# Four edits to a two-layer transformer kernel: a moved Silu, a projection that waits tile by tile, dots ahead of expert turns, and squares added in pairs

## The chip, the core and the metric

The kernel runs on one core of one Trainium2 chip. The metric is the device time of one execution in microseconds (us); lower is better. Everything is one launch, in fp32, with all inputs in HBM.

## The reference, cut

Two different transformer layers run one after the other on 256 tokens of width 1024. Each is modulated by a vector c: `silu(c) @ w_ada` gives shifts, scales and gates.

```python
# layer 1
sh1, sc1, gt1, sh2, sc2, gt2 = split(silu(c) @ w_ada + b_ada, 6)
proj = (rms_norm(h, norm1_g) * (1 + sc1) + sh1) @ w_in
...                                        # an attention (o_moba) and a recurrence (o_rwkv)
g_moba, g_rwkv = split(sigmoid(gate_logits), 2)
mixed = g_moba * (o_moba @ w_proj_moba) + g_rwkv * (o_rwkv @ w_proj_rwkv)
h = h + gt1 * (mixed @ w_out)
xn2 = rms_norm(h, norm2_g) * (1 + sc2) + sh2
h = h + gt2 * peer_ffn(xn2, ...)           # 8 heads choose 16 of 16384 experts per token:
                                           # gelu(x . u_e) * gate, times v_e, summed
# layer 2
shift_a, scale_a, gate_a, shift_f, scale_f, gate_f = split(silu(c_2) @ w_ada_2 + b_ada_2, 6)
h2 = rms_norm_2(x, attn_norm) * (1 + scale_a) + shift_a
...                                        # h2 @ w_in_2, two attentions, w_o, a convolved ffn
```

## The kernel before, in words

Five engines run queues that are written out by hand, in order: TensorE (`pe_...` functions), the Vector engine (`dve_...`), ScalarE (`act_...`), GpSimd (`pool_...`) and SP, which issues nearly all loads (`sp_...`). They meet in semaphores; `wait_ge` blocks the queue of its engine and `then_inc` raises a semaphore when the instruction is done. [...]

Weights come as tiles of 128 x 1024 in a ring of six slots (`wring`). Most products are made in three matmuls: ScalarE casts the upper half of a weight tile (L491, `whi`), the Vector engine or GpSimd subtracts it to get the lower half (L496, `wlo`), and TensorE multiplies upper by upper, upper by lower and lower by upper (L502 to L504). `tile_done` counts tiles that TensorE has finished, in one order for the whole program; `ring_free` counts PSUM banks (three in a ring) that have been read.

The places that the change touches, in the order of time:

- **Gates.** TensorE makes 16 gate tiles, the last of them beside the end of the recurrence. For each, ScalarE takes a sigmoid of the bank (L1340) and then casts the weight tile three further on. `act_rwkv_out` (L1719) does the last five; ahead of them it takes a square root (L1722) and the Silu of `crow` (L1726), the broadcast of c. Sqrt, Silu and Sigmoid each need a table load when they change. GpSimd subtracts for gate tiles 14 and 15.
- **Projections and output projection.** `pe_proj` makes eight tiles (L1742), `dve_proj` multiplies them with the gates and adds the two halves into `mix1` (L1762, L1764), and beside that takes dots of rows of `w_ada` with `crow` (L1781). `pe_w_out` waits until all eight tiles of `mix1` are there and then makes eight tiles (L477).
- **Experts.** All 16384 experts are computed densely, as 128 pairs of tiles: an up tile (L515 and L523, 16 + 8 matmuls) gives hidden values, and a down tile (L2106 to L2110, 12 matmuls) uses them. Up tiles 0 to 39 were made early. From j = 40 on a turn j is, on TensorE, up(j) and then down(j-1). On the Vector engine it is `turn(j)`: subtract the next up tile's lower half (L496), add the two parts of the hidden values (L2233), wait for ScalarE's Gelu, multiply by the gates (L2238), subtract the lower half of down tile j (L496), and subtract the lower part of W (L2226), which down(j) waits for. Turns 40 to 126 are two hardware loops of three turns each round; turn 127 stands alone.
- **Dots of layer 2's modulation.** Its 96 half rows (128 x 512, 256 KB) are loaded one by one into one buffer (`rG["half"]`, in `xn`), and the Vector engine takes a dot of each with crow2 (L2246, then a copy, L2249). `half(u)` waits for the landing of half u and gives the buffer free (`half_free`). Nine of them lie in the early down turns, the others one in each turn of the loops, u = 9 with j = 40 and so on. SP's queue in the loop (`sp_peer`) is, per turn, two weight tiles and one half:

```python
for u in range(SLOTS):
    tile(first + SLOTS + u, i)               # waits until the tile six back is done
    if u % 2:
        half(lone + u // 2 + 1, i)           # waits for half_free of the dot before
```

  Half 9 stands ahead of the loop, behind the weight tile that waits for down(38); half 10 behind the one that waits for down(39), and so on.
- **First norm of layer 2.** After the last down tile the residual is added in eight steps; for each, ScalarE writes the upper raw tile (L661) and a square (L547), the Vector engine the lower raw tile (L671), and TensorE takes six raw matmuls (two weight tiles of `w_in2`) and one norm matmul that sums the square over partitions into bank 4 (L576). Its result goes through a square root on ScalarE (L592) into all that follows. At the second norm of each layer GpSimd already adds squares (`pool_squares`, L567).

## Time and profile before

| | us |
|---|---|
| median of 3 runs | 1642.43 |
| lowest and highest run | 1640.56, 1642.7 |
| the profiled execution | 1641.95 |
| its span, first to last instruction | 1640.2 |
| TensorE busy in the span | 1599.8 (98%) |
| Vector engine busy | 1263.5 (77%) |
| ScalarE busy | 869.3 (53%) |
| GpSimd busy | 194.8 (12%) |

The expert loop, from 673 to 1156 us, is the longest stretch with one pattern. The gates end near 261 us, the two projections near 318, and the first norm of layer 2 lies from 1165 to 1176. In the views a row of the timeline is one group of equal instructions: start, duration, engine, line and operation; in brackets stands how long the engine was idle before it and what ended that.

### The profile page before, as it was taken

Reading aid. Unit: us, or ns where it says so; the run is one execution under the profiler, and the core shown is the slowest. Engines: PE = TensorE matmul, PEld = TensorE weight load, DVE = VectorE, ACT = ScalarE, POOL = GpSimd, SP = SyncE. Lnnn points to the kernel's source line nnn. Section 1 sums busy time; section 2 is a strip of 40 time slices with the busy share of each in tenths; the row PEclk is TensorE's granted clock in tenths of the full one; section 3 lists DMA queues with packets and bytes.
Section 4 is the critical chain, followed back from the end, with each engine's and each line's share of the span. In section 5 each row is a group of like instructions: output and inputs, shape, how many; then the busy total and the mean of one; then the engine's idle time right before and its main releaser. Section 6 shows DMA issues by size and latency. Waiting matters only on the chain.

```text
span 1640.2 us, 32822 instructions
## 1 busy us (share of the span) xinstructions
PE 1599.8 (98%) x11530; PEld 1421.0 (87%) x11530; DVE 1263.5 (77%) x2680; ACT 869.3 (53%) x1599; POOL 194.8 (12%) x153
## 2 busy tenths in 40 slices
PE   6999999999999999999999999999999999999998
PEld 4887988899988878888888888888899877999998
DVE  6885547859989978787888888888778465688887
ACT  3444221365469944555555555555654245566665
POOL 0020211017700000000000000000048004300000
PEclk9999999999999999999999999999999999999999
DMA  9842136855742288777767777777545561255553
GB/s 357 292 140 87 40 118 220 333 192 172 229 131 65 89 261 266 231 236 238 238 233 242 234 240 236 238 239 241 187 156 169 200 215 40 77 170 185 184 180 129
DMA packets 102625, 316.92 MB, mean 193 GB/s; under 512 B 11392, under 2 KB 21376, under 8 KB 102144
## 3 DMA queue, kind: packets, MB, share of 16 engines
q1 hardware_dynamic: 101664, 311.27, 57.2%
q10 hardware_dynamic: 864, 4.32, 0.7%
q8 instruction: 65, 1.06, 0.3%
q14 instruction: 32, 0.26, 0.0%
HBM read 309.65 MB, written 5.90 MB: 192 GB/s over the span
## 4 chain that ended last, share of the span: by engine, by line
PE 80%; ACT 7%; DVE 6%; POOL 2%; issue 2%; DMA 2%; SPq 0%; DVEq 0%; POOLq 0%; ACTq 0%
PE bank L515 10%; PE bank L502 9%; PE bank L503 8%; PE bank L504 8%; PE bank L2106 7%; PE bank L2108 7%; PE bank L2110 7%; PE bank L523 5%; POOL wlo L496 2%; ACT arena L2069 2%; PE bank L763 2%; PE bank L1624 2%; PE bank L1742 2%; ACT arena L2060 2%; PE bank L1325 1%
## 5 line engine op out<-in xcount | busy, mean ns | idle before, releaser
L491 ACT CAST whi<-wring 128x1024 fp32r<-128x1024 f32 x395 | 412.7, 1046 | 177.0 <-PE bank L504 109.6
L496 DVE TENSOR_TENSOR wlo<-wring,whi 128x1024 fp32r<-128x1024 f32 x341 | 416.9, 1223 | 63.8 <-ACT whi L491 55.0
L496 POOL TENSOR_TENSOR wlo<-wring,whi 128x1024 fp32r<-128x1024 f32 x54 | 138.1, 2564 | 910.3 <-ACT whi L491 910.3
L502 PE MATMUL bank<-xboth,whi 128*128 128x256 f32 x752 | 219.3, 292 | 6.8 <-POOL wlo L496 2.6
L503 PE MATMUL bank<-xboth,whi 128*128 128x256 f32 x752 | 212.6, 283 | 0.0
L504 PE MATMUL bank<-xboth,wlo 128*128 128x256 f32 x752 | 212.6, 283 | 0.0
L515 PE MATMUL bank<-xboth,whi 128*128 128x512 f32 x704 | 188.7, 390 | 0.0
L2106 PE MATMUL bank<-whi,Whi 128*128 128x512 f32 x512 | 159.7, 393 | 3.2 <-DVE Wlo L2226 3.2
L2108 PE MATMUL bank<-wlo,Whi 128*128 128x512 f32 x512 | 158.6, 391 | 0.0
L2110 PE MATMUL bank<-whi,Wlo 128*128 128x512 f32 x512 | 157.7, 389 | 0.0
L502 PEld LDWEIGHTS bank<-xboth,whi 128*128 128x128 f32 x752 | 143.9, 191 | 13.7 <-issue 6.4
L515 PEld LDWEIGHTS bank<-xboth,whi 128*128 128x128 f32 x704 | 132.5, 188 | 24.0
L502 PE MATMUL bank<-raw,whi 128*128 128x258 f32 x504 | 144.7, 287 | 2.9 <-DVE raw L671 1.4
L503 PEld LDWEIGHTS bank<-xboth,whi 128*128 128x128 f32 x752 | 144.1, 192 | 0.8 <-issue 0.7
L504 PEld LDWEIGHTS bank<-xboth,wlo 128*128 128x128 f32 x752 | 144.0, 191 | 0.0
L503 PE MATMUL bank<-raw,whi 128*128 128x258 f32 x504 | 142.8, 283 | 0.0
L504 PE MATMUL bank<-raw,wlo 128*128 128x258 f32 x504 | 141.5, 281 | 0.0
L2106 PEld LDWEIGHTS bank<-whi,Whi 128*128 128x128 f32 x512 | 95.2, 188 | 22.1 <-issue 2.9
L2110 PEld LDWEIGHTS bank<-whi,Wlo 128*128 128x128 f32 x512 | 96.1, 188 | 21.0
L2108 PEld LDWEIGHTS bank<-wlo,Whi 128*128 128x128 f32 x512 | 96.1, 188 | 21.0
L2179 ACT ACTIVATE arena<-arena 128x256 f32<-128x256 f32 x88 | 36.8, 418 | 128.1 <-DVE arena L2233 128.1
L523 PEld LDWEIGHTS bank<-xboth,wlo 128*128 128x128 f32 x704 | 96.0, 190 | 6.9
(397 smaller groups left out, 3111.7 us busy)
## 6 DMA issues: line engine op xcount, KB each, us to landing
wring<-in_w SPq DMA_DIRECT2D x463, 512.0 KB, 4.1
arena<-in_ada SPq DMA_DIRECT2D x48, 512.0 KB, 7.4
xn<-in_ada SPq DMA_DIRECT2D x96, 256.0 KB, 2.8
h_spill<-arena SPq DMA_DIRECT2D x37, 128.0 KB, 2.0
arena<-h_spill SPq DMA_DIRECT2D x37, 128.0 KB, 3.8
wring<-in_w SPq DMA_DIRECT2D x6, 384.0 KB, 6.0
wring<-in_w SPq DMA_DIRECT2D x8, 256.0 KB, 3.2
arena<-in_const ACTq DMA_DIRECT2D x1, 1151.0 KB, 5.3
```

The source lines that it names most:

```text
L491: act.copy(whi[:, n % HSLOTS, :], wring[:, n % SLOTS, :]).then_inc(hi_ready, 1)
L496: eng.tensor_tensor(wlo[:, n % SLOTS, :], wring[:, n % SLOTS, :], whi[:, n % HSLOTS, :].bitcast(F32), ALU.subtract).then_inc(lo_ready, 1)
L502: pe.matmul(out, h, xh, start=start, stop=False, **kw)
L503: pe.matmul(out, h, xl, start=False, stop=False, **kw)
L504: return pe.matmul(out, l, xh, start=False, stop=stop, **kw)
L515: return pe.matmul(out, whi[:, n % HSLOTS, k * 128:k * 128 + 128], xboth[:, k, :, :], start=(k == 0), stop=(k == KT - 1))
L523: pe.matmul(out[:, 0:S], wlo[:, n % SLOTS, k * 128:k * 128 + 128], xhi[:, k, :], start=False, stop=False)
L763: mm = pe.matmul(bk[:, at:at + w], q[:, b * 128:(b + 1) * 128], k[:, 0:w], start=(i == 0), stop=(i == len(j["q"]) - 1))
L2106: pe.matmul(tok_accs[b][f][:, :], Wh, h[:, f * 512:(f + 1) * 512], start=first, stop=False)
L2108: pe.matmul(tok_accs[b][f][:, :], Wh, l[:, f * 512:(f + 1) * 512], start=False, stop=False)
L2110: mm = pe.matmul(tok_accs[b][f][:, :], Wl, h[:, f * 512:(f + 1) * 512], start=False, stop=last)
L2179: act.activation(ge[:, j % 3, :], ge[:, j % 3, :], ACT.Gelu).then_inc(gelu_ready, 1)
```

## The change

Four places change. The Silu of `crow` moves behind the sigmoid of gate tile 13. `pe_w_out` waits, in its first tile, for one tile of `mix1` at a time. In the two loops of the expert stage the Vector engine takes the dot ahead of the turn instead of behind it, and in turn 127 it subtracts ahead of the add. At layer 2's first norm GpSimd adds the squares 0 and 1, 2 and 3, 4 and 5; TensorE takes three norm matmuls for the pairs and two for squares 6 and 7, and ScalarE's cast of `w_in2` tile 2 stands ahead of the last square. `sp_peer` is not touched.

```diff
+        DUOS = SUMMED // 2
+        SUMMED_AT = {1: SUMMED - 1, 3: 2 * (SUMMED - 1) + DUOS}
...
+        def pool_pairs(pool):
+            for i in range(DUOS):
+                pool.wait_ge(sq_ready, KT * 2 + 2 * i + 2)
+                pool.tensor_tensor(nsq[2][:, 2 * i, :], nsq[2][:, 2 * i, :], nsq[2][:, 2 * i + 1, :],
+                                   ALU.add).then_inc(sq_summed, 1)
+        def pair_sum(pe, i):
+            pe.wait_ge(sq_summed, SUMMED_AT[1] + i + 1)
+            pe.matmul(bank[NORM_BANK][:, 0:S], ones, nsq[2][:, 2 * i, :], start=(i == 0), stop=False)
...
         def act_rwkv_out(act):
...
-            act.wait_ge(crow_loaded, 32)
-            act.activation(rB["crow"], rB["crow"], ACT.Silu).then_inc(crow_ready, 1)
             for t in range(11, COUNT["gates1"]):
                 act_gates1(act, t, t + 1)
                 act_gate_hi(act, t + HSLOTS)
+                if t == CROW_AT:
+                    act.wait_ge(crow_loaded, 32)
+                    act.activation(rB["crow"], rB["crow"], ACT.Silu).then_inc(crow_ready, 1)
...
         def pe_w_out(pe):
-            pe.wait_ge(ring_free, RING0["w_out"])
-            ring_tiles(pe, "w_out", lambda slot, bk: matmul8(pe, bk[:, 0:S], slot, mix1),
-                       after=lambda k: k == KT - 1 and norm_summed(pe, 1))
+            first, ring0, mixed = FIRST["w_out"], RING0["w_out"], RING0["proj"]
+            for t in range(KT):
+                slot, bk = slot_of(first + t), bank[(ring0 + t) % BANKS]
+                pe.wait_ge(landed[slot], count_at(first + t))
+                pe.wait_ge(ring_free, ring0 + t - BANKS + 1)
+                for k in range(KT):
+                    if t == 0 and k >= KT - BANKS + 1:
+                        pe.wait_ge(ring_free, mixed + k + 1)
+                    mm = pe.matmul(bk[:, 0:S], blocks(slot, k), mix1[:, k, :], start=(k == 0), stop=(k == KT - 1))
+                mm.then_inc(tile_done, 1)
+            norm_summed(pe, 1)
...
         # pe_peer, the norm of layer 2
+                if k in (3, 5):
+                    pair_sum(pe, (k - 3) // 2)
+            pair_sum(pe, DUOS - 1)
+            for k in range(SUMMED, KT):
                 norm_sum(pe, 2, k, nsq[2])
...
         # act_peer
+                if m == KT - 1:
+                    act_hi_of(act, "w_in2", 2)
                 act_square(act, 2, m, nsq[2])
-            act_hi_of(act, "w_in2", 2)
...
         # dve_peer, turn(j)
-                if j < NK - 1:
-                    lo(n + 2, i)
+                lo(n + 2, i)
                 dve.wait_ge(h_rest, 3 * i + (j - EARLY + 1))
                 dve.tensor_tensor(ge[:, b, :], bank[j % 3][:, 0:S], ge[:, b, :], ALU.add).then_inc(h_summed, 1)
-                if j == NK - 1:
-                    lo(n + 2, i)
...
                     for j in range(EARLY, EARLY + 3):
+                        half(lone + j - EARLY, i, start > 0)
                         turn(j, i)
-                        half(lone + j - EARLY, i, start > 0)
```

On the Vector engine, at the top of the first expert loop, the rows before (`xn` holds the half row, `part` its dot, `mod` the kept value; `arena` is the hidden values):

```order
L2269 ISA
L496 TENSOR_TENSOR wlo<-wring,whi 128x1024 [waits hi_ready]
L2232 ISA
L2233 TENSOR_TENSOR arena<-bank,arena 128x256 [waits h_rest]
L2238 ISA [waits gelu_ready]
L2238 TENSOR_TENSOR arena<-arena 128x256
L495 REGISTER_ALU
L496 TENSOR_TENSOR wlo<-wring,whi 128x1024 [waits hi_ready]
L2225 REGISTER_ALU
L2226 TENSOR_TENSOR Wlo<-arena,Whi 128x256 [waits w_hi]
L2244 ISA
L2246 ISA xn,part<-xn,arena 128x512 [waits half_landed]
```

and the same place now (the dot's line is L2272, the add's L2261, the lower part of W L2255):

```order
L2295 ISA
L2272 ISA xn,part<-xn,arena 128x512 [waits half_landed]
L2272 ISA part 128x1
L2274 ISA
L2275 ISA [waits half_free]
L2275 COPY mod<-part 128x1
L495 ISA
L496 TENSOR_TENSOR wlo<-wring,whi 128x1024 [waits hi_ready]
L2260 REGISTER_ALU
L2261 TENSOR_TENSOR arena<-bank,arena 128x256 [waits h_rest]
L2264 ISA [waits gelu_ready]
L2264 TENSOR_TENSOR arena<-arena 128x256
```

The dot and its wait for `half_landed` moved from behind the lower part of W to ahead of the turn's first subtraction.

On ScalarE, at the last gate tiles, the rows before:

```order
L1722 ACTIVATE arena<-bank,cols 128x512
L1726 ACT_TABLE_LOAD
L1726 ACTIVATE arena<-arena 128x1024 [waits crow_loaded]
L1340 ACT_TABLE_LOAD
L1340 ACTIVATE arena<-bank 128x256 [waits tile_done]
L491 CAST whi<-wring 128x1024 [waits landed4]
L1340 ACTIVATE arena<-bank 128x256 [waits tile_done]
L491 CAST whi<-wring 128x1024 [waits landed5]
L1340 ACTIVATE arena<-bank 128x256 [waits tile_done] x3
```

and now (the sigmoid's line is L1353, the Silu's L1745):

```order
L1737 ACTIVATE arena<-bank,cols 128x512
L1353 ACT_TABLE_LOAD
L1353 ACTIVATE arena<-bank 128x256 [waits tile_done]
L491 CAST whi<-wring 128x1024 [waits landed4]
L1353 ACTIVATE arena<-bank 128x256 [waits tile_done]
L491 CAST whi<-wring 128x1024 [waits landed5]
L1353 ACTIVATE arena<-bank 128x256 [waits tile_done]
L1745 ACT_TABLE_LOAD
L1745 ACTIVATE arena<-arena 128x1024 [waits crow_loaded]
L1353 ACT_TABLE_LOAD
L1353 ACTIVATE arena<-bank 128x256 [waits tile_done] x2
```

The Silu with its table load moved behind the two casts and the third sigmoid; the number of table loads is the same.

On TensorE, in the last step of layer 2's first norm, the rows before and then now (L576 and L589 are the norm matmul of one square, L580 that of a pair):

```order
L502 MATMUL bank<-raw,whi 128x258
L503 MATMUL bank<-raw,whi 128x258
L504 MATMUL bank<-raw,wlo 128x258
L576 MATMUL bank<-arena,keep 128x256 [waits sq_ready]
L502 MATMUL bank<-raw,whi 128x258 [waits lo_ready]
```

```order
L502 MATMUL bank<-raw,whi 128x258
L503 MATMUL bank<-raw,whi 128x258
L504 MATMUL bank<-raw,wlo 128x258
L580 MATMUL bank<-arena,keep 128x256 [waits sq_summed]
L589 MATMUL bank<-arena,keep 128x256 [waits sq_ready] x2
L502 MATMUL bank<-raw,whi 128x258 [waits lo_ready]
```

Where one norm matmul stood at the end of each of eight steps, three now stand at the end of the last and one each after the fourth and the sixth.

## Rows read from the trace of the kernel before

**Rows 1.** The page: busy us, share, instructions of each engine; granted clock in 40 slices.
```profile
PE 1599.8 (98%) x11530; PEld 1421.0 (87%) x11530; DVE 1263.5 (77%) x2680; ACT 869.3 (53%) x1599; POOL 194.8 (12%) x153
...
PEclk9999999999999999999999999999999999999999
```

**Rows 2.** Timeline of TensorE, 236 to 335: start, us, instruction, [idle before <- releaser].
```profile
254.53 0.36 PE L502 MATMUL bank<-xboth,whi 128*128 128x256 f32 x1 [1.71 <-POOL wlo L496]
...
257.87 0.36 PE L502 MATMUL bank<-xboth,whi 128*128 128x256 f32 x1 [0.24 <-POOL wlo L496]
...
289.85 27.89 PE L477 MATMUL bank<-arena,wring 128*128 128x256 f32 x128 [1.24 <-DVE arena L1764]
```

**Rows 3.** Timelines of ScalarE and of GpSimd, same stretch.
```profile
246.96 1.28 ACT L1726 ACT_TABLE_LOAD   x1
...
249.33 1.28 ACT L1340 ACT_TABLE_LOAD   x1
...
252.02 5.70 POOL L496 TENSOR_TENSOR wlo<-wring,whi 128x1024 fp32r<-128x1024 f32 x2 [9.51 <-ACT whi L491]
```

**Rows 4.** Timeline of TensorE, first norm of layer 2.
```profile
1167.09 0.60 PE L576 MATMUL bank<-arena,keep 128*128 128x256 f32 x2
...
1167.64 0.28 PE L503 MATMUL bank<-raw,whi 128*128 128x258 f32 x1
1167.76 0.28 PE L504 MATMUL bank<-raw,wlo 128*128 128x258 f32 x1
...
1175.15 0.60 PE L576 MATMUL bank<-arena,keep 128*128 128x256 f32 x2
```

**Rows 5.** Timeline of the Vector engine: that norm, and three steps of other norms.
```profile
1165.67 0.48 DVE L671 SCALAR_TENSOR_TENSOR raw<-hT,gsc,raw 128x256 fp32r<-128x256 f32 x1
...
1166.46 0.48 DVE L671 SCALAR_TENSOR_TENSOR raw<-hT,gsc,raw 128x256 fp32r<-128x256 f32 x1
...
297.46 1.22 DVE L1781 CUSTOM_DVE_ANT_0 arena<-arena 128x1024 f32<-128x1024 f32 x1
...
298.60 1.74 DVE L1781 CUSTOM_DVE_ANT_0 arena<-arena 128x1024 f32<-128x1024 f32 x1
...
1432.98 0.57 DVE L671 SCALAR_TENSOR_TENSOR raw<-hT,gsc,raw 128x256 fp32r<-128x256 f32 x1
```

**Rows 6.** Timeline of TensorE, expert turns 40 and 41.
```profile
673.00 1.75 PE L515 MATMUL bank<-xboth,whi 128*128 128x512 f32 x7
...
678.51 1.75 PE L515 MATMUL bank<-xboth,whi 128*128 128x512 f32 x7
...
681.28 0.62 PE L2106 MATMUL bank<-whi,Whi 128*128 128x512 f32 x2
```

**Rows 7.** Timeline of SP's queue, same place: halves 9 and 10.
```profile
673.56 0.43 SPq L1007 DMA_DIRECT2D xn<-in_ada  x1
...
681.40 0.33 SPq L1007 DMA_DIRECT2D xn<-in_ada  x1
```

**Rows 8.** Loads of a half issued at 673.56, 1145.14, 597.79: KB, us to landing.
```profile
xn<-in_ada SPq DMA_DIRECT2D x1, 256.0 KB, 3.9
...
xn<-in_ada SPq DMA_DIRECT2D x1, 256.0 KB, 2.6
...
xn<-in_ada SPq DMA_DIRECT2D x1, 256.0 KB, 4.8
```

**Rows 9.** Timeline of the Vector engine, from the end of turn 40 through turn 41.
```profile
680.19 0.42 DVE L2226 TENSOR_TENSOR Wlo<-arena,Whi 128x256 fp32r<-128x256 f32 x1
680.53 0.68 DVE L2246 CUSTOM_DVE_ANT_0 xn<-xn,arena 128x512 f32<-128x512 f32 x1
...
681.47 1.23 DVE L496 TENSOR_TENSOR wlo<-wring,whi 128x1024 fp32r<-128x1024 f32 x1
...
685.60 0.42 DVE L2226 TENSOR_TENSOR Wlo<-arena,Whi 128x256 fp32r<-128x256 f32 x1
```

**Rows 10.** Timeline of TensorE, the last down tile.
```profile
1159.90 0.70 PE L2106 MATMUL bank<-whi,Whi 128*128 128x512 f32 x2 [0.83 <-DVE Wlo L2226]
```

More of the change, by code:

```diff
@@ L557, in build_layer_pair @@
         SUMMED = KT - 2
-        SUMMED_AT = {1: SUMMED - 1, 3: 2 * (SUMMED - 1)}
+        DUOS = SUMMED // 2
+        SUMMED_AT = {1: SUMMED - 1, 3: 2 * (SUMMED - 1) + DUOS}
         def pool_squares(pool, n):
@@ L1717, in pe_rwkv @@
             pe_gates1(pe, AT_END + 3, 128)
+        CROW_AT = 13
         def act_rwkv_out(act):
@@ L3245, in _ @@
             pool_route(pool)
+            pool_pairs(pool)
             pool.wait_ge(lo_ready, nth_split[FIRST["w_in2"] + RAW2 + 2])
```

## The prediction

> **What bounds the kernel now.** I read the page first: TensorE is busy 98% of the span, at a granted clock of nine tenths or more in every slice [rows 1]. So only what TensorE waits for, and what it executes, counts. Next I read its idle times in the stretches that the diff touches. Before the last two gate tiles it stands 1.71 and 0.24 us for GpSimd's lower half of the weights, and between the projections and the output projection 1.24 us for the last mixed tile [rows 2]. At the first norm of layer 2 it never waits between the squares; there it pays for eight norm matmuls [rows 4]. In the expert loop it has no idle at all: an up tile starts at 673.00 and the next at 678.51, so a turn is 5.51 us, of which down(40), from 681.28, leaves 2.77 us for the up tile and 2.74 for the down tile [rows 6]. The last thing to read is how far ahead of TensorE the Vector engine is in that loop: its last step of turn 40, the lower part of W, starts at 680.19 and takes 0.42 [rows 9], and TensorE takes it up at 681.28 [rows 6]. The slack is 0.67 us in a turn of 5.51. Whatever is put ahead of that step may delay it by no more than this.
>
> **Gates (Silu of crow moved behind gate tile 13).** Before, the Silu's table load starts at 246.96 and the sigmoid's at 249.33 [rows 3]: 2.37 us by which sigmoids 11 and 12, the two casts behind them and GpSimd's two subtractions (2.85 us each, from 252.02) come earlier. Both of TensorE's waits there (1.71 + 0.24 = 1.95 us) are for these subtractions; 2.37 covers the first, and the second subtraction then ends 2.37 us earlier too. Gain 1.95. The same 2.37 us of Silu and tables now lie between sigmoids 13 and 14, while TensorE computes tile 14 (24 matmuls that start 0.12 apart [rows 4], 2.9 us), and the first multiply that needs crow comes after the last gate. The price there is nothing.
>
> **Output projection.** It waited for all eight mixed tiles; now its first tile takes them one at a time and needs the eighth only at its eighth matmul, some 3 us after its first. That is longer than the 1.24 us [rows 2] for which the tile is late. Gain 1.24. What is late next is the dots of the second modulation; they move with the projection's tiles, since each waits for a slot that such a dot frees.
>
> **First norm of layer 2.** From the first to the eighth norm matmul it is 1175.15 - 1167.09 = 8.06 us for seven steps, 1.15 each [rows 4]; a step has six raw matmuls, which start 0.12 us apart (0.72) [rows 4], so one norm matmul costs 0.43. Eight become five: 1.29 us less. Against it, without norm matmuls in steps 0 to 3 TensorE would run at 0.72 a step while the Vector engine delivers raw tiles every 1166.46 - 1165.67 = 0.79 us [rows 5]; three steps at 0.07 give 0.2 back. Gain 1.1. GpSimd's three adds run beside the Vector engine, and the trace has both answers to whether that hurts: a dot took 1.74 us beside a GpSimd add where its neighbour took 1.22, but a raw tile's step beside one took 0.57 [rows 5] where it mostly takes 0.48. The norm's work is of the second kind, so I take 0.1 us at most; three adds at 0.52 would be 1.6 us, and the norm would lose 0.5.
> The Trainium skill (GPSIMD Engine Reference, section 1, Specifications) says that GpSimd shares its SBUF interfaces with VectorE and contends with instructions of two SBUF inputs. By that the raw steps, which have two, would be slowed as the dot is, and the norm's gain of 1.1 would turn into the loss of 0.5; the 0.57 us row speaks against it.
> The cast of w_in2 tile 2, now ahead of the last square, delays that square by one cast, about 1 us; TensorE asks for it only after the third pair, 2 us later. Nothing.
>
> **Expert loop.** This is the term that decides. In before, dot u of the second modulation comes after turn j; now it comes ahead of it, so on the Vector engine every dot, with its wait for the load of its half row, stands one turn earlier. The code that issues the loads is not changed. SP's queue holds, per turn, two weight tiles and then one half: half 9 stands behind the weight tile that waits for down(38) to end, half 10 behind the one that waits for down(39), half 11 behind down(40). In the trace, down(38) ends at 673.00 [rows 6] and half 9 is issued at 673.56 [rows 7]. In before this does not bind: half 10 is issued only at 681.40 [rows 7], after dot 9 (680.53) has freed the buffer [rows 9], and is wanted 5 us later. Now dot 9 is ahead of turn 40, dot 10 ahead of turn 41, and they are queued ahead of the whole turn. So there is a new ring:
> - down(j-2) ends, SP issues the half: 0.56 us [rows 6, 7]
> - the half lands: 3.9 us for this very load, right behind a weight tile [rows 8]
> - the dot with its read and copy, until the next subtraction: 681.47 - 680.53 = 0.94 [rows 9]
> - the turn up to the end of its lower part: 685.60 + 0.42 - 681.47 = 4.55 [rows 9]; it has two waits for ScalarE inside, which stay
> - two hand-overs, 0.14 together (my estimate, from the 0.18 us between the end of dot 9 at 681.22 and SP's issue at 681.40)
> - down(j): 2.74
> The sum is 12.83 us, and it spans two turns, for which TensorE needs 2 x 5.51 = 11.02. So two turns lose 1.81 us. The odd turns' ring starts 5.51 behind the even turns' and is never later than they are. From down(38) to down(126) there are 44 such pairs: 44 x 1.81 = +79.6 us. From this I take 1 us, which the loop of before already gives away in small delays behind the Vector engine: forecast +78.6.
> Bounds of the landing: 2.6 us for a half with no weight tile ahead, 4.8 for one behind a tile and beside spilled rows [rows 8]. They make the ring 11.53 and 13.73, the loop +22 and +118. I take 3.9: same place in the queue, same neighbours, and the tile ahead stays.
> The Trainium skill (DMA: Bandwidth & Descriptors, Anatomy of one DMA) gives a GpSimd-issued DMA 2.0 us plus its bytes at 436 GB/s. An estimate from that for tile and half together (786 KB) is 3.8 us from the tile's issue, some 0.5 before the half's, so 3.3 for the half; the row shows 3.9.
> **The last turn** now subtracts ahead of its add. In before TensorE stood 0.83 us there [rows 10], since the subtraction lay between add and multiply. Now the Vector engine arrives with nothing in hand, so the same subtraction lies on its path ahead of the add. Gain 0 to 0.5; I take 0.
>
> **Sum.** The profiled execution took 1641.95 us (span 1640.2), 0.5 under the median of 1642.43. 1641.95 - 1.95 - 1.24 - 1.1 + 78.6 = 1716.3: **1716 us**, 4.5% slower.
>
> **Rivals.**
> - *The loads keep ahead (faster).* If the half's load does not bind, the loop stays at 5.51 us a turn and only the 4.3 us of gain are left: 1637.7. It decides at issue plus landing of 2.65 us (11.02 less the other 8.37); the shortest in the trace are 0.56 + 2.6 = 3.16, and SP's order is fixed, so 0.07. This also stands for a change that does not do what it says.
> - *The load lands in 3.3 us*, between the two kinds of row, because a stretched loop has less traffic per us: ring 12.23, 44 x 1.21 = 53, so 1691. Chance 0.17. By the page named above the time would be this one.
> - *It lands in 2.6 us* as a lone half does: +22, 1660. Against it, the tile ahead shares the queue. 0.08.
> - *It lands in 4.8 us*: +118, 1756. For it only the stretch with spilled rows. 0.06.
> - A lower clock from the new idle would add to any of them; TensorE's idle of 1.71 us left the clock at nine tenths or more [rows 1, 2], so I give it no time.
>
> **How the numbers follow.** The forecast has 0.62 (its own range, landings of 3.6 to 4.3, 1703 to 1734). The range 1680 to 1740 takes in the forecast and the 3.3 us rival, 0.79, and a little of what lies beyond either. A measurement of this kernel can tell 0.2%, 3.3 us, from no change. Slower 0.93, faster 0.06 (the first rival at 1637.7 is 0.29% under the median), same 0.01.
>
> **What would show it.** In the changed kernel's expert loop: TensorE waits for the lower part of W in every second turn, 1.8 us, some 80 us in all; the Vector engine's dot waits for the load of the half; pairs of turns last 12.8 us; SP issues each half right after a weight tile, no longer after waiting for a dot. Waits for GpSimd ahead of gate tiles 14 and 15 gone; no wait ahead of the output projection; five norm matmuls. The prediction is wrong if a half lands within 2.1 us of its issue, or if SP's issue comes before the down tile's end.

## The result, and where the time went

The changed kernel takes 1722.59 us (median of 4 executions, 1721.19 to 1725.15) beside 1641.49 us for the kernel before on the same chip: a ratio of 1.0499, 95% interval 1.0486 to 1.0512. It is 5.0% slower. The forecast was 1716 us, with 1680 to 1740 as its range. The profiled execution of the changed kernel took 1725.15 us, its span is 1723.4; before, 1641.95 and 1640.2. Two later executions, one of the changed kernel (3201.82 us) and one of the kernel before (1766.38), fell in a slow state of the chip and are left out of every ratio and interval.

The whole loss lies in the expert loop. First the page of the changed kernel: the share of TensorE's busy time, and the row of its 40 slices.

```profile
PE 1621.9 (94%) x11524; PEld 1422.1 (83%) x11524; DVE 1268.9 (74%) x2680; ACT 866.5 (50%) x1600; POOL 196.8 (11%) x156
...
PE   6999999999999999889889988888999999999998
```

Before it was 98% [rows 1]. The eights between slices 17 and 28 lie in the loop. TensorE's work is the same but for a few norm matmuls, so a lower share means waits. The waits by engine say which: TensorE, the Vector engine and SP's queue of the changed kernel (engine, line, what it waited for: us in total, times, longest).

```profile
PE bank L2130 <- DVE Wlo L2255: 66.5, 55, 2.0
...
DVE xn L2272 <- DMA xn<-in_ada: 92.2, 71, 5.8
...
SPq L1016 <- PE bank L2134: 344.0, 124, 6.0
...
SPq L1020 <- DVE part L2272: 3.2, 3, 1.7
```

In the kernel before, SP waited for the dots instead (the same view):

```profile
SPq L1007 <- DVE part L2246: 193.3, 87, 4.6
```

Read the first of the two from the bottom. SP no longer waits for a dot before it issues a half (L1020: 3.2 us, 3 times; before, 193.3 us, 87 times), so the buffer is nearly always free when the half's turn comes; what SP waits for is the end of a down tile (L1016 on L2134). The Vector engine waits 92 us for the halves to land. TensorE waits 66.5 us for the lower part of W, in 55 places. One pair of turns shows the chain (timeline of all engines, rows left out):

```profile
1142.61 1.75 PE L515 MATMUL bank<-xboth,whi 128*128 128x512 f32 x7
...
1142.95 0.33 SPq L1016 DMA_DIRECT2D wring<-in_w  x1
1143.53 0.33 SPq L1020 DMA_DIRECT2D xn<-in_ada  x1
...
1147.08 0.69 DVE L2272 CUSTOM_DVE_ANT_0 xn<-xn,arena 128x512 f32<-128x512 f32 x1 [1.81 <-DMA xn<-in_ada]
...
1148.05 1.23 DVE L496 TENSOR_TENSOR wlo<-wring,whi 128x1024 fp32r<-128x1024 f32 x1
1148.16 1.75 PE L515 MATMUL bank<-xboth,whi 128*128 128x512 f32 x7
...
1152.17 0.42 DVE L2255 TENSOR_TENSOR Wlo<-arena,Whi 128x256 fp32r<-128x256 f32 x1
...
1152.65 0.73 PE L2130 MATMUL bank<-whi,Whi 128*128 128x512 f32 x2 [1.56 <-DVE Wlo L2255]
...
1155.50 0.84 PE L515 MATMUL bank<-xboth,whi 128*128 128x512 f32 x3
```

A down tile ends at 1142.61, where the next up tile starts. SP issues the weight tile that waited for it 0.34 later and the half 0.92 later; the dot starts 3.55 after that; 0.97 for the dot; 4.54 from the subtraction at 1148.05 to the end of the lower part; TensorE starts down at 1152.65 and the pair ends at 1155.50. That is 12.89 us for two turns; the median of the 43 stalled pairs is 12.98. Before, two turns took 11.03.

One more thing is in the trace, which the prediction named and gave no time. TensorE's granted clock, by stretches (columns: stretch, its length, busy time of PE, PEld, DVE, ACT, POOL, granted clock, DMA share, GB/s):

```profile
681.00:685.00 4.00, 4.00 (x13) 3.13 (x12) 3.21 (x5) 1.66 (x3) 0.00 (x0) 0.57 0.08 29
685.00:689.00 4.00, 4.00 (x23) 3.44 (x22) 0.60 (x2) 1.43 (x2) 0.00 (x0) 1.00 0.57 206
708.00:712.00 4.00, 3.66 (x9) 2.91 (x10) 3.22 (x7) 1.36 (x3) 0.00 (x0) 0.59 0.30 116
1087.00:1091.00 4.00, 4.00 (x12) 3.15 (x11) 3.05 (x6) 1.81 (x4) 0.00 (x0) 0.57 0.11 45
```

In three places the clock stands at 0.5 (its level of 1.2 GHz) for some 3.4 us, each behind one of the longest waits (1.97, 1.82 and 1.75 us), and in between at 1.00; the shares of 0.57 and 0.59 are means of stretches that hold some full clock too. The same kind of tile shows it in the timeline: a group of two matmuls takes 1.06 us at 682.16 and 0.62 at 687.56.

```profile
680.34 0.70 PE L2130 MATMUL bank<-whi,Whi 128*128 128x512 f32 x2 [1.97 <-DVE Wlo L2255]
...
682.16 1.06 PE L2130 MATMUL bank<-whi,Whi 128*128 128x512 f32 x2
...
687.56 0.62 PE L2130 MATMUL bank<-whi,Whi 128*128 128x512 f32 x2
```

At half the clock 3.4 us cost 1.7, so the three places cost 5.1 us. The kernel before has no such stretch in its loop.

**The account.** From the start of turn 40 to the start of the last down tile the changed kernel takes 1245.08 - 668.59 = 576.49 us, the kernel before 1159.90 - 673.00 = 486.90: +89.6. Of this 43 pairs at 12.98 - 11.03 = 1.95 make 83.9, the clock 5.1, and the first pair, which takes 16.13 with 1.7 of the clock in it (its dot starts at 674.68, 5.53 us after the half's issue at 669.15), 1.5 more. The rest (-0.9) is the last down tile's wait, 0.38 instead of 0.83 [rows 10], and small delays in the loop before, whose 43 pairs take 474.88 us where those of experiment 3, which has no wait there, take 474.15. Outside the loop: -3.9 in the gates and projections, -1.1 from the last down tile through the norm, and -1.4 in pieces of 0.2 to 0.9 that belong to no edit. The sum is +83.2, the difference of the spans.

### The profile page after: what moved, and what is told of

Same layout as the page of the kernel before. It is cut to its first block, busy times and chain, and to the rows that moved or that the text cites. A ratio compares the mean times of both kernels' runs of the same rounds, so it can differ in the third digit from the quotient of the medians.

```text
span 1723.4 us, 32814 instructions
## 1 busy us (share of the span) xinstructions
PE 1621.9 (94%) x11524; PEld 1422.1 (83%) x11524; DVE 1268.9 (74%) x2680; ACT 866.5 (50%) x1600; POOL 196.8 (11%) x156
## 3 DMA queue, kind: packets, MB, share of 16 engines
q8 instruction: 65, 1.06, 0.3%
## 4 chain that ended last, share of the span: by engine, by line
PE 56%; DMA 11%; issue 11%; DVE 9%; ACT 9%; POOL 2%; SPq 2%; DVEq 0%; ACTq 0%; POOLq 0%
DMA xn<-in_ada 9%; PE bank L502 8%; PE bank L503 8%; PE bank L504 8%; PE bank L2130 5%; PE bank L2134 4%; PE bank L2132 4%; ACT whi L491 3%; ACT arena L2093 2%; PE bank L776 2%; PE bank L1637 2%; PE bank L1758 2%; POOL wlo L496 2%; ACT arena L2084 2%; DVE wlo L496 2%
## 5 line engine op out<-in xcount | busy, mean ns | idle before, releaser
L2130 PE MATMUL bank<-whi,Whi 128*128 128x512 f32 x512 | 169.1, 412 | 67.0 <-DVE Wlo L2255 66.5
L2130 PEld LDWEIGHTS bank<-whi,Whi 128*128 128x128 f32 x512 | 90.3, 189 | 105.7 <-DVE Wlo L2255 84.7
L2134 PE MATMUL bank<-whi,Wlo 128*128 128x512 f32 x512 | 160.1, 394 | 0.0
L504 PEld LDWEIGHTS bank<-xboth,wlo 128*128 128x128 f32 x752 | 144.0, 192 | 0.0
L2272 DVE CUSTOM_DVE_ANT_0 xn<-xn,arena 128x512 f32<-128x512 f32 x96 | 66.4, 691 | 92.7 <-DMA xn<-in_ada 92.2
L2134 PEld LDWEIGHTS bank<-whi,Wlo 128*128 128x128 f32 x512 | 97.1, 190 | 21.6
```

The source lines that it names most:

```text
L504: return pe.matmul(out, l, xh, start=False, stop=stop, **kw)
L2130: pe.matmul(tok_accs[b][f][:, :], Wh, h[:, f * 512:(f + 1) * 512], start=first, stop=False)
L2134: mm = pe.matmul(tok_accs[b][f][:, :], Wl, h[:, f * 512:(f + 1) * 512], start=False, stop=last)
L2272: dve.tensor_tensor_reduce(rG["half"], rG["half"], c, 1.0, 0.0, ALU.mult, ALU.add, part[:, u % 3:u % 3 + 1]).then_inc(half_free, 1)
```

## Experiments

The theory: a ring of two turns, in which a half can be issued only behind the weight tile that waits for down(j-2), and its dot now stands ahead of turn j. The main rival: the dot's place on the Vector engine costs the loop, since 0.94 us of work now lies ahead of the lower part of W where there was 0.67 of slack, wherever the load is issued.

**1. The dot behind its turn again, everything else kept.**

```diff
                     for j in range(EARLY, EARLY + 3):
-                        half(lone + j - EARLY, i, start > 0)
                         turn(j, i)
+                        half(lone + j - EARLY, i, start > 0)
```

> The changed kernel with one edit undone: in the expert loop each dot stands behind its turn again. The ring theory (a half can only be issued when down(j-2) has ended, and its dot stands ahead of turn j) has the whole loss in this edit: the loop goes back to 11.03 us per two turns and the other edits' gains stay, about 4.3 us by the working of the prediction and 5.6 by the trace of the changed kernel: 1636 to 1637.5 us. If the loss came from the other edits (output projection, norm, last turn), it would stay near 1722. TensorE's wait for the lower part of W: under 5 us in all, against 66.5.

Measured: 1636.25 us, ratio to the kernel before 0.9957 (0.9943 to 0.9971). Pairs of turns are back at 11.03. The whole loss hangs on this one edit, and without it the other edits leave the kernel 0.4% faster than before.

**2. This edit alone, on the kernel before.**

```diff
                     for j in range(EARLY, EARLY + 3):
+                        half(lone + j - EARLY, i, start > 0)
                         turn(j, i)
-                        half(lone + j - EARLY, i, start > 0)
```

> The kernel before with this edit alone: the dot ahead of its turn. The ring theory: pairs of turns of 12.9 to 13.1 us against 11.03, 43 of them, +84 and a few us at the loop's entry: 1726 to 1730 us, some 5 us above the changed kernel, which has the small gains besides. If the edits depend on each other, the difference to the changed kernel is not those 5 us.

Measured: 1735.78 us, ratio 1.0571 (1.0555 to 1.0588). The edit alone makes the loss; but it is 13 us above the changed kernel's median, not 5. The trace has pairs of 13.05 at the median, and the clock at its lower level in two places, which cost 3.4 us. The changed kernel itself ran from 1724 to 1744 us on other chips (experiment 7), so what lies beyond the 5 says nothing about the edits.

**3. Dots ahead, but SP issues every half one turn (two weight tiles) earlier.**

```diff
                 if j + 4 in LONE_HALVES:
                     half(LONE_HALVES.index(j + 4), 0)
+                if j + 3 == EARLY:
+                    half(len(LONE_HALVES), 0)
...
-            half(lone, 0)
             with sp.Fori(0, end) as i:
                 for u in range(SLOTS):
+                    if u % 2 == 0:
+                        half(lone + u // 2 + 1, i)
                     tile(first + SLOTS + u, i)
-                    if u % 2:
-                        half(lone + u // 2 + 1, i)
```

(The halves behind the loop move up likewise.)

> The changed kernel, dots ahead of their turns as they are; only SP's queue differs: every half of the loop is issued two weight tiles (one turn) earlier, so that it stands behind the weight tile that waits for down(j-3). The ring theory: what binds is then only the single buffer, dot j-1 end, 0.2 us to SP's issue, 3.5 to 3.9 landing, 0.95 dot: 4.7 to 5.1 us in a turn of 5.51, so the loads keep ahead and TensorE no longer waits: 1635 to 1639 us, SP waiting for a dot at most halves. The rival (the dot itself, 0.94 us ahead of the lower part of W where the Vector engine has 0.67 us of slack, costs the loop, wherever the load is issued): 0.27 us in each of 88 turns, 1660 us, or no change from 1722.

Measured: 1634.99 us, ratio 0.9956 (0.9943 to 0.997). The rival falls: the dot stands where the change put it, and the loop runs at 11.03 us per pair without a wait. Two turns of it, with SP's issue of a half and the dot that reads it:

```profile
1138.39 1.75 PE L515 MATMUL bank<-xboth,whi 128*128 128x512 f32 x7
...
1140.38 0.33 SPq L1020 DMA_DIRECT2D xn<-in_ada  x1
...
1143.91 1.75 PE L515 MATMUL bank<-xboth,whi 128*128 128x512 f32 x7
...
1145.17 0.68 DVE L2274 CUSTOM_DVE_ANT_0 xn<-xn,arena 128x512 f32<-128x512 f32 x1
...
1149.42 1.75 PE L515 MATMUL bank<-xboth,whi 128*128 128x512 f32 x7
```

The half issued at 1140.38 has landed when the dot at 1145.17 wants it (no idle in front of it). This version and the first both beat the kernel before; between the two no difference is measured. Why the dot itself costs nothing can be read off the diff of experiment 2: inside the loop the Vector engine's order is turn, dot, turn, dot in either kernel. What the edit changes is which half the dot between two turns reads: the next one, which SP has only just issued.

**4. The mirror image: dots behind their turns as before, SP's halves one turn later.**

```diff
                 for u in range(SLOTS):
                     tile(first + SLOTS + u, i)
                     if u % 2:
-                        half(lone + u // 2 + 1, i)
+                        half(lone + u // 2, i)
```

(The half ahead of the loop goes, and the last two tiles' halves move down likewise.)

> The mirror image: the kernel before, dots behind their turns as they were, but SP issues every half of the loop two weight tiles (one turn) later, behind the tile that waits for down(j-1). The ring theory sees the same ring as in the changed kernel (issue 0.9, landing 3.5, dot 0.95, a turn 4.55, down 2.75: 12.9 us per two turns): 1722 to 1732 us. The rival, for which the dot's place on the Vector engine is what costs: no change, 1640 to 1646 us.

Measured: 1741.19 us, ratio 1.0606 (1.0586 to 1.0626), pairs of 13.29. With the Vector engine's order untouched, the same loss comes back. It is the distance between a half's place in SP's queue and its dot's place in the Vector engine's that costs, and it doesn't matter which of them is moved. It lies 9 us above the expected range; its profiled execution has 6.8 us of lower clock, in four places, and halves that land in 3.7 us instead of 3.6.

**5. A shorter load in the same ring.** Each half of the loop brings a quarter of its columns, and the dot is scaled by 1/16: the kernel leaves three quarters of the loaded rows out of the second modulation, and every engine's work stays.

```diff
-                sp.dma_start(rG["half"], a["ada2"][3 * i + u]).then_inc(half_landed, 16)
+                w = AHALF if u < len(LONE_HALVES) else AHALF // 4
+                sp.dma_start(rG["half"][:, 0:w], a["ada2"][3 * i + u][:, 0:w]).then_inc(half_landed, 16)
...
-                dve.tensor_tensor_reduce(rG["half"], rG["half"], c, 1.0, 0.0, ALU.mult, ALU.add,
+                dve.tensor_tensor_reduce(rG["half"], rG["half"], c, 1.0 / 16, 0.0, ALU.mult, ALU.add,
```

> The changed kernel, but each load of a half in the loop brings only a quarter of its columns (64 KB instead of 256 KB); the dot reads the whole buffer as before (a quarter of it fresh, the rest what the last dot left, scaled by 1/16 so that it stays small), so the second modulation is wrong and the work on every engine the same. Only the landing is shorter. By the ring theory the loop changes by 43 times the change of the landing: 0.3 to 1.2 us less landing (a 64 KB load still stands behind a 512 KB tile) gives 1671 to 1710 us, my value 0.6 less, 1697; pairs of turns shorter by exactly what the landing is shorter. If the dot's place on the Vector engine were the cause, the bytes would not matter: 1722.

Measured: 1705.22 us, ratio 1.0388 (1.0372 to 1.0404); pairs of 12.61. The loads in the loop, this run and then the changed kernel (KB each, median us from issue to landing):

```profile
xn<-in_ada SPq DMA_DIRECT2D x83, 64.0 KB, 3.2
```

```profile
xn<-in_ada SPq DMA_DIRECT2D x85, 256.0 KB, 3.6
```

The landing is 0.4 us shorter and the pair 12.98 - 12.61 = 0.37: the ring passes on what the landing loses, 43 x 0.37 = 16 us. The medians differ by 17.4, which agrees only roughly: the two kernels ran on different chips, the changed kernel's time holds stretches at the lower clock and a longer first pair, and this one has neither. The guess of what three quarters of the bytes are worth (0.6) was too high. Size is the small part of this landing.

**6. The weight tile ahead of the half.** The half waits for the same down(j-2) but is issued ahead of the tile; SP's loop is written out for it.

```diff
-            with sp.Fori(0, end) as i:
+            for i in range(end):
                 for u in range(SLOTS):
-                    tile(first + SLOTS + u, i)
                     if u % 2:
+                        n = first + SLOTS + u
+                        sp.wait_ge(tile_done, SLOTS * i + (n - SLOTS + 1))
                         half(lone + u // 2 + 1, i)
+                    tile(first + SLOTS + u, i)
```

> The changed kernel, dots ahead; only the order of two neighbours in SP's queue differs: each half waits for the same down(j-2), but is issued ahead of the weight tile that waits for it, not behind (SP's loop is written out for it, with constants in its waits). So the ring stays, and loses what the tile ahead puts into it: the tile's own place in SP's issue (0.34 us of 0.92) and its share of the landing (3.5 us behind a tile; 2.8 is the median in the kernel with the dots behind their turns, where a half has no tile right ahead of it). Expected pairs of turns: 12.9 - 0.34 - 0.75 = 11.8 us, 43 x 1.1 = 47 us less than the changed kernel, 1675. If the landing doesn't depend on the tile ahead: 43 x 0.34 = 15 less, 1708. A time of 1636 would mean that the place in the queue, not the ring, was what counted.

Measured: 1653.73 us, ratio 1.0085 (1.0053 to 1.0117); pairs of 11.32. The gain is larger than expected: both terms shrank further.

```profile
1103.30 1.75 PE L515 MATMUL bank<-xboth,whi 128*128 128x512 f32 x7
...
1103.50 0.33 SPq L1020 DMA_DIRECT2D xn<-in_ada  x1
...
1106.21 0.69 DVE L2274 CUSTOM_DVE_ANT_0 xn<-xn,arena 128x512 f32<-128x512 f32 x1 [0.18 <-DMA xn<-in_ada]
```

```profile
xn<-in_ada SPq DMA_DIRECT2D x83, 256.0 KB, 2.6
```

The half is issued 0.20 after the down tile's end (0.92 in the changed kernel) and lands in 2.6 (3.6). The ring is still there, 0.3 us per pair over TensorE's own 11.03. On this chip the profiled execution of the changed kernel took 1739.47 us (experiment 7) and the kernel before 1641.68 at the median: of a loss of 98 us 86 are gone by swapping two neighbours in SP's queue, in a loop written out (what the writing out is worth is the next run).

**7. SP's loop written out, order unchanged,** beside **the changed kernel once more**, on one chip; and the changed kernel on another chip, that of experiment 6.

```diff
-            with sp.Fori(0, end) as i:
+            for i in range(end):
```

> The changed kernel with SP's loop in the expert loop written out (every wait and every load with constants), its order unchanged: two weight tiles, then a half. It separates what the half-first kernel mixed: there SP's loop was written out too. The prediction took 0.56 us from the end of down(j-2) to the half's issue from half 9, the one half that SP issues ahead of its loop; inside the loop the changed kernel takes 0.92. If the loop's registers make the difference, the issue comes back to 0.55 to 0.6, pairs of turns get 0.35 shorter, and the time is 43 x 0.35 = 15 us below the changed kernel on the same chip. If not, no difference between the two.

> The changed kernel, unchanged, as the measure for the run beside it on the same chip: 1720 to 1745 us, the upper end where the granted clock falls in many turns (eight places of 1.7 us in the run before).

> The changed kernel once more, unchanged, for the scatter of its stalled loop and of the granted clock: 1719 to 1727 us; in the profile down tiles at the lower clock in 0 to 5 places, 1.6 us each, always behind one of TensorE's longest waits.

Measured: written out 1721.59 us (ratio 1.0484, 1.0464 to 1.0504), the changed kernel beside it 1726.15 (1.0531, 1.0507 to 1.0555), and on the other chip 1732.9 to 1744.1 in three executions (1.0593, 1.0546 to 1.0641). Writing out brought 4.5 us, not the 15 expected:

```profile
1106.17 1.75 PE L515 MATMUL bank<-xboth,whi 128*128 128x512 f32 x7
...
1106.36 0.33 SPq L1016 DMA_DIRECT2D wring<-in_w  x1
...
1106.73 0.43 SPq L1020 DMA_DIRECT2D xn<-in_ada  x1
...
1110.55 0.69 DVE L2272 CUSTOM_DVE_ANT_0 xn<-xn,arena 128x512 f32<-128x512 f32 x1 [1.54 <-DMA xn<-in_ada]
```

```profile
xn<-in_ada SPq DMA_DIRECT2D x85, 256.0 KB, 3.9
```

The issue did come back to 0.56 us, but the landing went to 3.9: 4.46 together, against 0.92 + 3.6 = 4.52 in the first run of the changed kernel and 0.9 + 3.7 = 4.6 in the one beside this. The half is issued sooner behind the tile but hardly lands sooner. The pairs, 12.95 against 13.05 on the same chip, make 43 x 0.10 = 4.3 us of the 4.5. In experiment 6, with no tile ahead, the sum was 0.20 + 2.6 = 2.8. So 1.66 us of every ring is the 512 KB tile in front of the half, and the pairs say the same: 12.95 against 11.32, though on two chips.

The run on the other chip lies above its expected 1719 to 1727. Part of it is the clock: eight stretches of its profiled execution look like this one, where 0 to 5 were expected, and they cost 13.6 us:

```profile
695.00:699.00 4.00, 4.00 (x12) 3.14 (x11) 3.00 (x6) 1.28 (x2) 0.00 (x0) 0.57 0.19 78
```

The other part is the ring itself: its pairs take 13.17 us at the median, 0.19 more than in the first run, with halves that land in 3.7 us, and 43 x 0.19 = 8 us.

**8. The three small edits, each alone on the kernel before.** The Silu behind gate tile 13 (the diff of `act_rwkv_out` and nothing else):

> The kernel before with the Silu of crow behind gate tile 13, nothing else. Prediction: TensorE's two waits for GpSimd's lower half of the weights (1.71 and 0.24 us) go, minus 1.95 us. By the trace of the changed kernel, where the clock of the program is 4.2 us ahead after the output projection, this and the next edit share 4.2: minus 2 to 3. 1638.5 to 1640.

Measured: 1638.83 us, ratio 0.9981 (0.9972 to 0.999).

The output projection's waits per mixed tile (the diff of `pe_w_out` and nothing else):

> The kernel before with the output projection's waits per mixed tile, nothing else. Prediction: the wait of 1.24 us for the last mixed tile goes, minus 1.24; by the trace of the changed kernel up to minus 2. 1639.5 to 1640.5. If GpSimd or the dots of the second modulation are late next, the wait comes back at the next tiles and the time stays.

Measured: 1639.32 us, ratio 0.9989 (0.998 to 0.9998).

The norm in five matmuls (`pool_pairs`, `pair_sum`, their calls, and the cast moved ahead of the last square):

> The kernel before with the norm in five matmuls and GpSimd's three adds (and the cast of w_in2 tile 2 ahead of the last square), nothing else. Prediction: minus 1.1 us; the trace of the changed kernel says 1.05: 1640.5 to 1641. If GpSimd slowed the Vector engine's raw steps as it slows a dot (1.74 against 1.22 us), plus 0.5. The trace decides, by the steps beside an add (0.57 in the changed kernel, 0.48 alone).

Measured: 1639.03 us, ratio 0.9987 (0.9978 to 0.9996).

Each gains about two us at the median, with intervals that reach from 0.3 to 4.6. The projection's and the norm's times lie 0.2 and 1.5 us below what was expected of them; the intervals are too wide to tell whose part that is. The traces can, because they show the same stretch without the rest of the program. TensorE's waits of the run with the Silu alone, and then of the run with the projection alone:

```profile
287.33 27.89 PE L477 MATMUL bank<-arena,wring 128*128 128x256 f32 x128 [1.24 <-DVE arena L1767]
316.29 0.36 PE L502 MATMUL bank<-raw,whi 128*128 128x258 f32 x1 [0.63 <-DVE wlo L496]
```

```profile
254.88 0.36 PE L502 MATMUL bank<-xboth,whi 128*128 128x256 f32 x1 [1.71 <-POOL wlo L496]
258.22 0.36 PE L502 MATMUL bank<-xboth,whi 128*128 128x256 f32 x1 [0.23 <-POOL wlo L496]
317.65 0.36 PE L502 MATMUL bank<-raw,whi 128*128 128x258 f32 x1 [0.63 <-DVE wlo L496]
```

Each edit takes away its own waits of [rows 2] and leaves the other's. Measured from ScalarE's square root ahead of both edits (245.67 before, 245.55 and 246.02 in these two, 245.37 in the changed kernel) to the wait of 0.63 or 0.64 at the end, the stretch takes 73.14 us before, 70.74 with the Silu moved (-2.40), 71.63 with the projection's waits (-1.51) and 69.24 in the changed kernel (-3.90, their sum).

## The prediction, step by step

**Right: the mechanism.** TensorE waits for the lower part of W, the Vector engine's dot for the half, SP's queue for the down tile and no longer for the dot; experiments 1 to 4 leave no other cause. The forecast of 1716 is 6.6 us under the median. On the chips of experiment 7 the same kernel took 1726.15 us at the median and 1732.9 to 1744.1, so one execution lies above the range.

**The ring: 12.83 forecast, 12.98 measured**, with two terms wrong that nearly cancelled. The issue is 0.92, not 0.56: [rows 7] shows half 9, the one half that SP issues ahead of its loop, with constants; inside the loop each issue takes longer. The landing is 3.6, not 3.9. Experiment 7 shows why the sum held (4.46 there, 4.46 in the prediction): both were read off the same half, and behind a tile a half's arrival hangs on the tile, not on its own issue. A landing from one row and an issue from another would have been off by 0.3 us, 13 us in the total. The down tile took 2.85 instead of 2.74 where TensorE had waited.

**The signs: waits of 1.8 us in every second turn, some 80 us forecast; 66.5 us in 55 places measured.** Some pairs split their stall between both turns. And the idle time is not the whole price: the last of these matmuls ahead of a wait takes 0.39 us where neighbours start 0.23 apart, and the down tile behind it 0.11 more. An estimate from this is 0.27 a wait, 66.5 + 55 x 0.27 = 81 of the 84 us that the pairs lost.

**The count: 44 pairs forecast, 43 stalled.** Behind SP's loop one half follows each of the last two weight tiles, where inside the loop one follows every second tile. So the last half is issued ahead of the end of down(124), at 1233.53, and its dot, at 1235.98, waits for nothing (SP's queue of the changed kernel):

```profile
1231.28 0.33 SPq L1020 DMA_DIRECT2D xn<-in_ada  x1
```

The 1 us that the prediction took off for small delays in the loop before was about right: it is 474.88 - 474.15 = 0.73.

**Wrong: the clock got no time.** The prediction inferred from one wait of 1.71 us [rows 2] that waits of about this length leave the clock alone. In the stalled loop waits of 1.74 to 1.97 us were followed by 3.4 us at 1.2 GHz in some of their places: 1.7 us each, 5.1 in the profiled execution, 1.7 and 13.6 in the two others. The page could not have warned of it: one of its 40 slices is 41 us long, and the kernel before has such a fall too, behind a wait of 2.46 us near its start, in a slice that reads nine tenths or more:

```profile
23.24:26.65 3.41, 3.41 (x6) 1.34 (x5) 3.40 (x6) 0.10 (x1) 0.00 (x0) 0.50 1.02 407
```

This term belongs to the sum, with its own width; it is most of what the forecast lacks beside the 4 us of the ring.

**Wrong by little: the loop's entry.** The first half's dot came 5.53 us after the issue, where issue to dot is 3.55 later on, and the first pair took 16.13. In the two other profiled executions of the same kernel that pair took 13.39 and 13.03, so its size is the execution's, not the kernel's.

**Gates and projection: 3.19 forecast, 3.90 measured.** Both waits went and nothing came in their place. The size was short because an idle time in the trace begins at the last matmul's end, and without a wait the next one starts before that. The matmul ahead of the first wait and the second one behind it, in the kernel before:

```profile
252.54 0.28 PE L504 MATMUL bank<-xboth,wlo 128*128 128x256 f32 x1
...
254.72 0.28 PE L503 MATMUL bank<-xboth,whi 128*128 128x256 f32 x1
```

From start to start that is 2.18 us where two steps of 0.12 would have done: the wait costs 1.94, not its idle 1.71. Of the 0.23 more, 0.16 is the lost overlap of the last matmul, and 0.07 lies in the first one behind the wait, which holds the next off for 0.19. The same reckoning gives 0.47 for the wait of 0.24 and 1.51 for that of 1.24: 3.92 together, against the 3.90 measured.

**The norm: 1.1 forecast, 1.05 measured.** TensorE's norm matmuls and GpSimd's adds in the changed kernel, then the Vector engine's raw steps:

```profile
1254.63 0.59 PE L580 MATMUL bank<-arena,keep 128*128 128x256 f32 x2
...
1258.38 0.60 PE L580 MATMUL bank<-arena,keep 128*128 128x256 f32 x2
1258.82 1.03 PE L589 MATMUL bank<-arena,keep 128*128 128x256 f32 x4
```

```profile
1251.78 0.90 POOL L574 TENSOR_TENSOR arena<-arena 128x256 f32<-128x256 f32 x1 [808.59 <-ACT arena L547]
1253.41 0.95 POOL L574 TENSOR_TENSOR arena<-arena 128x256 f32<-128x256 f32 x1 [0.73 <-ACT arena L547]
```

```profile
1251.61 0.48 DVE L684 SCALAR_TENSOR_TENSOR raw<-hT,gsc,raw 128x256 fp32r<-128x256 f32 x1
1252.39 0.57 DVE L684 SCALAR_TENSOR_TENSOR raw<-hT,gsc,raw 128x256 fp32r<-128x256 f32 x1
```

From the first raw step to the end of the last norm matmul it is 1259.85 - 1250.82 = 9.03 us, before 1175.75 - 1165.67 = 10.08 [rows 4, 5]; alone (experiment 8) it gains the same. A raw step that starts while an add runs takes 0.57 instead of 0.48, as in [rows 5]; one that starts ahead of the add keeps its 0.48. The Trainium skill (GPSIMD Engine Reference, section 1, Specifications) has GpSimd contend with such instructions; the trace agrees that it does, and puts the price at 0.09 us a step here, not at the 0.52 that a dot paid.

**The last turn: 0 forecast (0 to 0.5), 0.45 measured**: TensorE's wait for the last lower part is 0.38 where it was 0.83 [rows 10]. With the dots behind the turns again (experiment 1) it is 0.83 as before, and with the dots ahead but the old order inside the last turn (experiment 2) it is 0.82. TensorE's timeline there, of the changed kernel, then of experiment 1 and of experiment 2:

```profile
1245.08 0.70 PE L2130 MATMUL bank<-whi,Whi 128*128 128x512 f32 x2 [0.38 <-DVE Wlo L2255]
```

```profile
1158.12 0.70 PE L2130 MATMUL bank<-whi,Whi 128*128 128x512 f32 x2 [0.83 <-DVE Wlo L2255]
```

```profile
1251.25 0.70 PE L2106 MATMUL bank<-whi,Whi 128*128 128x512 f32 x2 [0.82 <-DVE Wlo L2226]
```

So the gain needs both edits, and neither brings it alone. With the dot gone from ahead of the last turn, the Vector engine stands idle ahead of the add (0.87 us in experiment 2), and the subtraction moved there fills that time. The prediction put the last turn at nothing because the subtraction would stay on the path.

**The rivals.** "The loads keep ahead" needed SP's order to change; experiment 3 did that and got 1635 against the 1637.7 worked out. "3.3 us" did not occur. The Trainium skill (DMA: Bandwidth & Descriptors, Anatomy of one DMA) has its formula from GpSimd-issued DMAs; these are SP's. An estimate from it is 3.8 us for tile and half together; from the tile's issue to the dot it is 1147.08 - 1142.95 = 4.13, 0.3 more. For a half alone the estimate is 2.6, and in experiment 6 the half with no tile ahead lands in 2.6. "2.6 us" as a rival had the right number for the wrong place: it holds for a half with no tile in front.

## What to carry to other kernels

When a consumer of loaded data moves one turn earlier, its load has to move one place earlier in the queue that issues it; otherwise a queue order that never bound becomes a ring, and its price is (issue + landing + consumer + turn + producer) minus the turns it spans, times the number of rounds. A small load that someone waits for belongs ahead of a large one that nobody waits for yet: here two neighbours swapped were worth 68 us (1721.59 to 1653.73, both with SP's loop written out, on two chips) of a loss of 80, and a place one turn earlier in the queue was worth all of it (experiment 3). And a wait on TensorE costs more than its idle: the overlap of the last matmul each time, and in this case now and then 3.4 us at half the clock.

## What was not expected of the hardware

- In the stalled loop TensorE's granted clock fell to 0.5 for about 3.4 us at waits of 1.74 to 1.97 us, and rose again by itself while TensorE worked on. It did not fall at every wait of that length (the changed kernel's second pair has one of 1.87 us without it), nor in the loop with pairs of 12.61 us, whose waits reach 1.5. How often differs between executions and chips: 1, 3 and 8 places in three profiled executions of the same kernel. What decides it stays open.
- A half behind a 512 KB tile of the same queue lands 4.5 to 4.6 us after the event that both wait for, whether SP issues it 0.56 or 0.92 us after that event.
- With a quarter of the bytes a landing behind that tile is only 0.4 us shorter (3.2 instead of 3.6).
- In SP's loop with registers the first load is issued 0.34 us after the event and the second 0.58 after the first; written out with constants it is 0.19 and 0.37.
- A small add on GpSimd stretched a raw step that starts beside it on the Vector engine from 0.48 us to 0.57, and a dot of 1.22 us to 1.74 [rows 5].
